# Layer 0 of a four-layer block: the attention of dilation 16 taken from TensorE to GpSimd and VectorE

## The reference, cut to what matters

```python
DSA_PATTERNS = ((128, 1), (512, 4), (2048, 16))        # window, dilation
def dilated_mixer(x, w_in, w_out, cos, sin):
    h = x @ w_in
    ...
    for g, (window, dilation) in enumerate(DSA_PATTERNS):
        q = apply_rope(qkv[:, :, g, 0], cos, sin)
        k = apply_rope(qkv[:, :, g, 1], cos, sin)
        o, l = dilated_window_attention(q, k, qkv[:, :, g, 2], window, dilation)
    ...
    wts = jax.nn.softmax(jnp.stack(lses, axis=0), axis=0)
    o = jnp.einsum('gbsh,gbshd->bshd', wts, jnp.stack(outs, axis=0).astype(jnp.float32))
    y = o.reshape(B, S, DSA_WIDTH).astype(x.dtype) * jax.nn.silu(z)
    return y @ w_out
```

## Time and profile before

| | |
|---|---|
| median of 3 runs | 2406.14 us (2406.0 to 2406.15) |
| span of the profiled execution, first to last instruction | 2404.2 us |
| PE busy in that span | 2395.8 us |
| DVE busy | 1478.8 us (62%) |
| ACT busy | 1186.4 us (49%) |
| POOL busy | 151.6 us (6%) |
| granted TensorE clock | 1.000 |

### The profile page before, as it was taken

How to read it: one execution, slowest core, us unless ns; L and a number is a source line. 1 busy time by engine, 2 the same in 40 slices (tenths; PEclk the granted TensorE clock), 3 DMA queues, 4 the chain that set the end, 5 groups by cost and what they waited for, 6 DMA issues and landing times.

```text
span 2404.2 us, 31347 instructions
## 1 busy us (share of the span) xinstructions
PE 2395.8 (100%) x12574; PEld 2043.6 (85%) x12574; DVE 1478.8 (62%) x1986; ACT 1186.4 (49%) x1645; POOL 151.6 (6%) x130
## 2 busy tenths in 40 slices
PE   9999999999999999999999999999999999999999
PEld 8888888888888888878899878888888888888887
DVE  6747575757575757575556576555445566757754
ACT  5454444444444444445455456455444358745543
POOL 0201010101010101000000000000000010000000
PEclk9999999999999999999999999999999999999999
DMA  8555555555555555556654556556555565534344
GB/s 265 178 173 191 196 185 169 186 168 186 168 186 169 186 167 176 194 164 201 188 142 136 193 160 201 179 178 193 177 178 171 175 196 172 157 120 128 126 140 140
DMA packets 370366, 418.26 MB, mean 174 GB/s; under 512 B 28262, under 2 KB 300876, under 8 KB 369708
## 3 DMA queue, kind: packets, MB, share of 16 engines
q1 hardware_dynamic: 368876, 409.36, 53.3%
q0 software_dynamic: 1344, 6.89, 0.8%
HBM read 414.09 MB, written 2.11 MB: 173 GB/s over the span
## 4 chain that ended last, share of the span: by engine, by line
PE 97%; DVE 1%; ACT 1%; issue 0%; POOL 0%; DVEq 0%; ACTq 0%; POOLq 0%
PE ps L696 19%; PE ps L698 19%; PE ps L697 19%; PE ps L730 15%; PE ps L729 7%; PE ps L1260 2%; PE ps L771 2%; PE ps L983 1%; PE ps L972 1%; PE ps L1037 1%; PE ps L1035 1%; PE ps L1036 1%; PE ps L977 1%; PE ps L802 1%; PE ps L804 0%; PE ps L803 0%
## 5 line engine op out<-in xcount | busy, mean ns | idle before, releaser
L2030 DVE TENSOR_TENSOR wlo<-raw,whi 128x1024 fp32r<-128x1024 f32 (+1 forms) x756 | 938.6, 1251 | 617.8 <-ACT whi L1387 615.0
L1387 ACT CAST whi<-raw 128x1024 fp32r<-128x1024 f32 x762 | 789.1, 1041 | 713.8 <-PE ps L698 536.1
L696 PE MATMUL ps<-whi,xx 128*128 128x512 f32 x2060 | 820.3, 398 | 0.0
L698 PE MATMUL ps<-whi,xx 128*128 128x512 f32 x2060 | 803.6, 390 | 0.0
L697 PE MATMUL ps<-wlo,xx 128*128 128x512 f32 x2060 | 802.2, 389 | 0.0
L730 PE MATMUL ps<-xx,whi 128*128 128x512 f32 x1536 | 539.4, 396 | 0.0
L698 PEld LDWEIGHTS ps<-whi,xx 128*128 128x128 f32 x2060 | 386.7, 188 | 82.5
L697 PEld LDWEIGHTS ps<-wlo,xx 128*128 128x128 f32 x2060 | 387.5, 188 | 75.5
L696 PEld LDWEIGHTS ps<-whi,xx 128*128 128x128 f32 x2060 | 387.2, 188 | 74.5
L729 PE MATMUL ps<-xx,wlo 128*128 128x256 f32 x1440 | 406.0, 282 | 0.0
L730 PEld LDWEIGHTS ps<-xx,whi 128*128 128x128 f32 x1536 | 286.3, 188 | 63.2 <-DVE wlo L2030 0.3
(11 more groups left out here) (436 smaller groups left out, 1917.1 us busy)
## 6 DMA issues: line engine op xcount, KB each, us to landing
raw<-in_dsa_w_in SPq DMA_DIRECT2D x316, 512.0 KB, 4.5
raw<-in_ev_w_in SPq DMA_DIRECT2D x144, 512.0 KB, 4.6
raw<-in_od_w_in SPq DMA_DIRECT2D x96, 512.0 KB, 4.6
raw<-in_mla_w_in SPq DMA_DIRECT2D x48, 512.0 KB, 4.5
raw<-in_dsa_w_out SPq DMA_DIRECT2D x32, 512.0 KB, 4.7
raw<-in_mla_w_out SPq DMA_DIRECT2D x32, 512.0 KB, 4.8
raw<-in_ev_w_out SPq DMA_DIRECT2D x32, 512.0 KB, 4.7
raw<-in_od_w_out SPq DMA_DIRECT2D x32, 512.0 KB, 4.9
```

The source lines that it names most:

```text
L696: pe.matmul(o, xh[:, k, tokens[tb]], hi, start=start and s + l == 0, stop=False)
L698: m = pe.matmul(o, xl[:, k, tokens[tb]], hi, start=False, stop=stop and s + l == 2)
L1387: act.copy(half_of_weights(h)[0][:, :, 0:n] if n > FEW else few_high(h, n), whole_half(raw[:, u % 4, 2 * (h % 2):2 * (h % 2) + 2], n)).the ...
L2030: dve.tensor_tensor(lo[:, :, 0:n] if n > FEW else few_low(h, n), whole_half(raw[:, h // 2 % 4, 2 * (h % 2):2 * (h % 2) + 2], n), hi.bitcas ...
```

## The change

Group 2 (dilation 16) no longer goes through PE's attention.

- Its q, k and v for all heads are made first, as twelve product slabs of rows (`row` 0 to 11, half of the heads in six of them), between the first block and the second of pair 0. q and k are rotated as rows on DVE (`row_ropes`: two products with the sines of 128x512, one with the cosines and one sum of 128x1024). SP stores every row slab to DRAM (`far_rows`) and loads it back with a partition for each residue and head (`far_q`, `far_k`, `far_v`; both half of the heads at a time).
- For each of two halves of the heads and each lag from 0 to 15, POOL multiplies q with the k of lag positions before, 128 x (16 - lag) x 128 elements, and DVE reduces over the 128. After maximum, exponential and sum POOL multiplies v by the weight of each lag, in the same sizes, and DVE adds lags 1 to 15 into `far_o`. The output, and the negated scaled maximum and sum (`ext`), are stored and loaded back by token into `y` and `near_ext`.
- PE's attention keeps groups 0 and 1: four blocks to a pair, four score matmuls, six transposes and six matmuls with v to a head. Each head takes the far part in by maximum and sum (`attend0`, `fin`).
- z is made for two pairs in one product. All of a rotation of turned q and k is on DVE; POOL has none of it.
- Far work is taken forward by its own step count (`joined`). A lag's place is set by `lag_steps`: 0.39 steps for each 128 elements.

```diff
-ROWS_AT = (40, 44, 48, 52)
+ROWS_AT = (104, 108, 112, 116)
+
+STEPS0 = (256, 48, 64, 48, 64, 48, 64, 48)
+ROPE_AT = (226,) + 7 * (31,)
+LAGS = 16
+ROW_ROPE_AT = (34, 43, 58, 74, 122, 138, 154, 170)
+FAR_AT = (100, 246)
+STORES_AT = {16: 0, 18: 1, 22: 2, 26: 3, 30: 4, 34: 5, 38: 6, 42: 7, 46: 8, 50: 9, 54: 10, 58: 11}
+FAR_LOADS_AT = (27, 64)
+FAR_VALUES_AT = (46, 82)
+FAR_STORES_AT = (61, 97)
+FAR_BACK_AT = (63, 99)
+
+
+def lag_steps(lag):
+
+    return math.ceil(sum(LAGS - j for j in range(lag + 1)) * 0.39) + 1
...
+def joined(n, side, more):
+
+    for _ in range(n):
+        next(side, None)
+        next(more, None)
+        yield
+    yield from side
...
-            h = c(10, TB, HALF)
+            h = c(6, TB, HALF)
+            hz = c(TB, N)
             t1, t2 = c(2, S), c(2, S)
             cosr, sinr = t1, t2
-            qk = c(6, 2, S)
-            vb = c(3, TB, HALF)
+            qk = c(4, 2, S)
+            vb = c(2, TB, HALF)
             zs = c(TB, HALF)
-            sm, pt, mask = c(TB, N), c(TB, N), c(TB, N)
+            sm, pt, mask = c(TB, 3 * P), c(TB, 3 * P), c(TB, 3 * P)
+            tmp = [c(LAGS, P), c(LAGS, P)]
+            far_s, far_p = c(LAGS, LAGS), c(LAGS, LAGS)
+            far_m, ext, near_ext = c(LAGS), c(LAGS, 2), c(TB, 16, 2)
+            evicted = [by_token(h[:, 1:3]), by_token(h[:, 3:5])]
+            rows = [by_token(qk[:, 0:2]), by_token(qk[:, 2:4])]
+            far_q, far_k = [x[:, n].rearrange("p (i d) -> p i d", d=P) for n in range(2)]
+            far_v, far_o = far_k, far_q
...
+        slabs0 = [("block", 0, 0)] + [("row", i, None) for i in range(12)]
+        for pair_ in range(8):
+            slabs0 += [("block", pair_, n_) for n_ in range(0 if pair_ else 1, 4)]
+            slabs0 += [("z", pair_ // 2, None)] * (pair_ % 2 == 0) + [("v", pair_, None)]
...
+                if u in STORES_AT:
+                    i = STORES_AT[u]
+                    sp.wait_ge(*(rr_d.at(L0.ROPED.index(i), "r") if i in L0.ROPED else row_a.at(0, f"row{i}")))
+                    sp.dma_start(far_rows[L0.KINDS[i], i // 6].rearrange("(p t) c -> p t c", t=TB)[:, :, i % 2 * N:(i % 2 + 1) * N],
+                                 L0.rows[i % 2]).then_inc(rows_stored[i % 2], 16)
+                for half in range(2):
+                    if u == FAR_LOADS_AT[half]:
+                        sp.wait_ge(*xt_p.at(7, "t"))
+                        if half:
+                            sp.wait_ge(far_stored, 32)
+                        for kind, dst in ((0, L0.far_q), (1, L0.far_k)):
+                            for e in range(2):
+                                sp.wait_ge(rows_stored[e], 16 * (2 + 3 * half))
+                            sp.dma_start(dst, by_sequence_of(far_rows[kind, half])).then_inc(far_in, 16)
+                    if u == FAR_VALUES_AT[half]:
+                        sp.wait_ge(*far_g.at(half, "q15"))
+                        for e in range(2):
+                            sp.wait_ge(rows_stored[e], 16 * (3 + 3 * half))
+                        sp.dma_start(L0.far_v, by_sequence_of(far_rows[2, half])).then_inc(farv_in, 16)
+                    if u == FAR_STORES_AT[half]:
+                        sp.wait_ge(*far_d.at(half, "a14"))
+                        sp.dma_start(by_sequence_of(far_out[half]), L0.far_o).then_inc(far_stored, 16)
+                        ext = far_ext[half]
+                        sp.dma_start(bass.AP(ext.tensor, ext.offset, [[2, P], [2 * P, LAGS], [1, 2]]), L0.ext) \
+                            .then_inc(far_stored, 16)
+                    if u == FAR_BACK_AT[half]:
+                        sp.wait_ge(far_stored, 32 * (half + 1))
+                        sp.wait_ge(*setup_p.at(0, "vec"))
+                        sp.dma_start(y[:, :, half * 1024:(half + 1) * 1024], far_out[half].rearrange("(p t) c -> p t c", t=TB)) \
+                            .then_inc(far_back, 16)
+                        sp.dma_start(L0.near_ext[:, :, 8 * half:8 * half + 8],
+                                     far_ext[half].rearrange("(p t) h e -> p t h e", t=TB)).then_inc(far_back, 16)
...
-                            for g in range(3):
+                            for g in range(2):
...
-                        for b in range(8):
-                            m = pe.transpose(flat4[:, b * P:(b + 1) * P], L0.sm[:, b // 4, b % 4 * P:(b % 4 + 1) * P], ident[:, :])
+                        for b in range(6):
+                            m = pe.transpose(flat4[:, b * P:(b + 1) * P], L0.sm[:, b // 3, b % 3 * P:(b % 3 + 1) * P], ident[:, :])
...
-                            for b, (g, kb) in enumerate(((0, 0), (0, 1), (1, tb), (2, tb))):
+                            for b, (g, kb) in enumerate(((0, 0), (0, 1), (1, tb))):
                                 m = pe.matmul(ps[:, Q + 3, tokens[tb]], L0.pt[:, tb, b * P:(b + 1) * P],
-                                              L0.vb[:, g, kb, hh * P:(hh + 1) * P], start=b == 0, stop=b == 3)
+                                              L0.vb[:, g, kb, hh * P:(hh + 1) * P], start=b == 0, stop=b == 2)
...
+            def attend0(h, last):
+                mx, nb, den, rden = head_scales(h)
+                rel, more = far_scales(h)
+                act.wait_ge(*hd_d.at(h, "nb"))
+                for tb in range(TB):
+                    m = act.activation(L0.sm[:, tb], L0.sm[:, tb], ACT.Exp, bias=nb[:, tb:tb + 1], scale=P ** -0.5,
+                                       accum_out=den[:, tb:tb + 1])
+                m.then_inc(*hd_a.up("exp"))
+                act.wait_ge(*w0_d.at(h, "rel"))
+                act.activation(rel, rel, ACT.Exp).then_inc(*w0_a.up("w"))
...
+                elif kind == "row":
+                    if i in L0.ROPED:
+                        e = L0.ROPED.index(i)
+                        if e >= 2:
+                            act.wait_ge(*rr_d.at(e - 2, "r"))
+                        dst = L0.evicted[e % 2]
                     else:
-                        if pair:
-                            act.wait_ge(*p0_d.at(pair - 1, "z"))
-                        act.copy(L0.h[:, 8], ps[:, b:b + 2, 0:HALF])
-                        act.activation(L0.h[:, 9], ps[:, b:b + 2, HALF:N], ACT.Copy, scale=0.5).then_inc(*e0_a.up("out7"))
-                run(side)
+                        act.wait_ge(rows_stored[i % 2], 16 * (i // 2))
+                        dst = L0.rows[i % 2]
+                    act.copy(dst, ps[:, b:b + 2, :]).then_inc(*row_a.up(f"row{i}"))
...
-                for n in range(6):
+                for n in range(4):
                     dve.wait_ge(*s0_d.at(pair, f"sum{n}"))
...
                     for a_, b_ in ((slice(0, 64), slice(64, P)), (slice(64, P), slice(0, 64))):
                         m = dve.tensor_tensor(L0.t2[a_], L0.h[b_, n], bc(L0.sina[b_], 1, 2), ALU.mult)
                     m.then_inc(*p0_d.up(f"t{n}"))
-                    dve.wait_ge(*p0_d.at(pair, f"t{n}"))
-                    dve.wait_ge(*p0_g.at(pair, f"cos{n}"))
+                    dve.tensor_tensor(L0.t1, L0.h[:, n], bc(L0.cosa, 1, 2), ALU.mult).then_inc(*p0_d.up(f"c{n}"))
+                    dve.wait_ge(*p0_d.at(pair, f"c{n}"))
                     dve.tensor_tensor(L0.qk[:, n], L0.t1, L0.t2, ALU.add).then_inc(*p0_d.up(f"r{n}"))
                     yield
...
+            def row_ropes():
+                to = steps()
+                for e, i in enumerate(L0.ROPED):
+                    src, dst = [v.rearrange("p t (h d) -> p t h d", d=P) for v in (L0.evicted[e % 2], L0.rows[i % 2])]
+                    cos_, sin_ = [bc(v[:, :, 0:P], 2, 4) for v in (L0.cosr, L0.sinr)]
+                    yield from to(ROW_ROPE_AT[e])
+                    dve.wait_ge(*row_a.at(0, f"row{i}"))
+                    if e == 0:
+                        dve.wait_ge(*rope_a.at(0, "raw"))
+                    if i >= 2:
+                        dve.wait_ge(rows_stored[i % 2], 16 * (i // 2))
+                    for o, n in ((slice(0, 64), slice(64, P)), (slice(64, P), slice(0, 64))):
+                        m = dve.tensor_tensor(dst[:, :, :, o], src[:, :, :, n], sin_[:, :, :, n], ALU.mult)
+                    m.then_inc(*rr_d.up("t"))
+                    dve.wait_ge(*rr_d.at(e, "t"))
+                    dve.tensor_tensor(src, src, cos_, ALU.mult).then_inc(*rr_d.up("c"))
+                    yield
+                    yield
+                    dve.wait_ge(*rr_d.at(e, "c"))
+                    dve.tensor_tensor(dst, dst, src, ALU.add).then_inc(*rr_d.up("r"))
+
+            def far0():
+                to = steps()
+                for half in range(2):
+                    begin = FAR_AT[half]
...
+                    for lag in range(LAGS):
+                        yield from to(begin + lag_steps(lag))
+                        dve.wait_ge(*far_g.at(half, f"q{lag}"))
+                        dve.tensor_reduce(L0.far_s[:, lag:, lag], L0.tmp[lag % 2][:, 0:LAGS - lag], AX.X, ALU.add) \
+                            .then_inc(*far_d.up(f"s{lag}"))
```

(83 more changed lines are left out.)

223 lines of the change are left out of this document (139 added, 84 removed).

## The result

The changed kernel takes 2446.77 us (median of 4 runs, 2445.61 to 2447.6); in the same session the kernel before took 2406.14. The ratio is 1.0169, 95% interval 1.0154 to 1.0183: slower by 40.6 us. The direction is the one that was forecast, the size is not: 2446.8 lies above the forecast of 2418.2 and above the range's end of 2436.

What follows compares the result with a forecast made beforehand. PE was taken to bound the kernel. Span 2404.2 - 22.7 of PE work + 19.3 + 15.5 of standstill in the output phases = 2416.3, or 2418.2 us as a median of runs; range 2382 to 2436.

Steps and rivals of the forecast that it cites:

- PE's gain, 22.7 us: PE's work: 17.6 us less in sixteen heads, 5.1 us from 16 blocks becoming 8 products; with nothing late, 2383.4 us.
- What the meeting costs: POOL and DVE instructions with two SBUF inputs don't overlap: POOL keeps DVE out 2.1 ns an element, 37.8 us a phase.
- I take no meeting: DVE's reductions, with one SBUF input, were taken not to meet POOL at the port; 19.7 us of reductions a phase.
- It fits: Both score phases: port work of 79.8 us in 80.2 and 83.5 in 86.3, so no standstill of PE.
- Reductions contend too, 2443: Rival: reductions also meet POOL, score phases add 13.5 + 11.1 us of standstill; chance 0.12 together with weights late.
- The outputs: Output phases: port work over the time by 25.1 and 21.3 us; less the slack, PE stands still 19.3 and 15.5 us.
- The clock: Rival: PE's clock falls to 1.2 GHz in an output phase, 70 us more, 2488 us; chance 0.04.
- PE at 98% keeps 1.00: Evidence cited on the clock rival: in the rows PE busy at 98% keeps full clock; nothing lower is shown.
- Weights late: Rival: weights queue behind SP's far transfers, 0 to 5 us, to 2423; beyond 2428, chance 0.12 together with contending reductions.
- The signs: Listed observations that would show the forecast right or wrong, among the wrong ones PE idle in a score phase.
- the band of 2428 to 2445: Outcome band for the whole kernel if reductions contend or weights come late; chance 0.12.
- The faster rival: Rival: the port doesn't bind, DVE gets in between parts of POOL's long instructions, nothing is late; 2383.4 us, faster 0.30.

Runs made afterwards that it cites:

- sp_late: The changed kernel with SP storing rows 8 to 11 at units 48, 52, 55 and 59 instead of 46, 50, 54 and 58: 2442.2 us.
- the pieces: The changed kernel with each POOL product cut into instructions of at most 128x512, nothing left out: 2425.7 us.

## Why the prediction was wrong

- **PE's gain, 22.7 us**: right. 2382.7 measured with the far arithmetic cut, 2383.4 forecast; a head gives 1.12 for 1.10, later pairs take 73.1 and 94.9 us for 73.2 and 94.9.
- **What the meeting costs**: right in kind. A split that meets a long product stands until it ends (4.4 us for 1.18), additions too. Mis-sized for the two kinds: 2.25 and 1.78 ns an element for 2.1; a phase of scores is 17408 x 2.25 = 39.2 us, one of outputs 31.0, for 37.8 each. DVE's prices were a little low: 0.69 us for a rotation's instruction of 128x512, counted at 0.61 although has 692 ns, and 20.4 us of reductions a phase for 19.7.
- **"I take no meeting" for the reductions**: right as to the port (the 128x1024 form takes 1210 ns here, as it does before with nothing beside it), and it is also what the Trainium skill says (SBUF — State Buffer, "Who interferes with whom"): an exclusive lock for the whole instruction, and a `tensor_reduce` stays outside it. The trace agrees with both, by 4.4 us for a split of 1.18 and by these 1210 ns.
- **"It fits", 79.8 us of port work in 80.2 and 83.5 in 86.3: the step that failed.** It counted the port alone, as if the reductions lay beside products. Once DVE is late they don't: a product starts when a reduction frees its buffer, DVE's splits then stand behind the product, the next reduction behind the splits, and POOL waits for that. The right budget of a score phase is in series, port work and reductions: 79.8 + 19.7 = 99.5 us for 80.2. With them cut, 26.0 us come back. PE stands still for 7.3 + 17.9 = 25.2 us in the score phases, where nothing was forecast. The rival "Reductions contend too, 2443" had this sum, by a mechanism that the rows refute. Its 13.5 + 11.1 = 24.6 us match the 25.2 in sum only; by halves it is 7.3 and 17.9, so the near hit is in part luck.
- **The outputs**: forecast 34.8 us of standstill, measured 18.2 of idle time and some of the slower clock. v came late, as said: POOL's first output product starts at 264.1 us, after 23 us of waiting for it. The difference is mostly the price, 6.8 us a phase less than counted: with it the prediction's own sum gives 34.8 - 13.6 = 21.2 us.
- **The clock**: a rival with a chance of 0.04 and 70 us; it did fall, for some microseconds behind seven standstills and not for a whole phase. All told the loss is 2446.8 - 2382.7 = 64.1 us, 43.4 of it idle time of PE and the other 20.7 longer busy time, of which the clock makes 13.6. The remaining 7 us were not taken apart. "PE at 98% keeps 1.00" was no evidence for stretches with standstills of several microseconds.
- **Weights late**: in the range of 0 to 5 us that was given. ACT waits 18.9 us for them, 8.1 at once; 14.0 us of such waits, 4.2 at once, are there without the far arithmetic too and cost nothing. What DVE's lateness adds to SP's waits is worth about the 4.6 us of sp_late, one run.
- **The signs**: of those named as wrong, three came: a score phase with PE idle, ACT's cast ended by a DMA, a clock below 1.00. The first is the one that points at the step that failed.

The sum that would have come out: 22.7 us of gain, 34.8 of standstill as forecast, 24.6 for reductions in series gives 2442.8; the measured 2446.8 is that with 16.6 less in the outputs and 20.7 more of longer busy time, two misses that nearly cancel. It lies above the band of 2428 to 2445, which had a chance of 0.12. That chance and the range's end at 2436 were too small for a single assumption, reductions beside products, that the nearest row supported only for the port. The faster rival, DVE getting in between parts of a long product, didn't occur: it gets in between instructions, as the pieces show.

## What to carry to other kernels

Work for GpSimd that hands its buffers back and forth with VectorE must be budgeted in series with all that VectorE has queued, not by the shared port alone. If VectorE also feeds the engine that bounds the kernel, cut GpSimd's instructions well below the time that this feed can be late (here 128x512, 21 us better with the same arithmetic), and stretch the work over more steps until VectorE's sum, its waits for GpSimd included, fits with a margin. A long wait in a trace is not yet a loss: compare it with a kernel that leaves the work out. A standstill of TensorE can cost more than its length, since its clock fell behind seven of them here.
